# A decoder layer on one core: the diagonal scores and the first score level taken by one series of products

## The reference, cut to what matters

```python
def step(S, inp):
    qc, kc, vc, gc = inp
    b = jnp.cumsum(gc, axis=2)
    o_inter = jnp.einsum('bhtk,bhkv->bhtv', qc * jnp.exp(b), S)
    diff = b[:, :, :, None, :] - b[:, :, None, :, :]
    decay = jnp.where(causal, jnp.exp(jnp.where(causal, diff, 0.0)), 0.0)
    scores = jnp.einsum('bhtk,bhsk,bhtsk->bhts', qc, kc, decay)
    o = o_inter + jnp.einsum('bhts,bhsv->bhtv', scores, vc)
    ...
```

## Time and profile before

| | |
|---|---|
| median of three runs | 1082.59 us |
| the profiled execution's own time | 1080.87 us |
| its span | 1079.1 us |
| TensorE matmul busy | 1051.9 us (97%) |
| VectorE busy | 674.0 us (62%) |
| ScalarE busy | 478.9 us (44%) |
| mean granted clock of TensorE | 0.996 of full |
| first diagonal product | 67.53 us from the start |
| last L255 matmul of the four rounds | 598.8 us |

### The profile page before, as it was taken

How to read it: one execution, slowest core, us unless ns; L and a number is a source line. 1 busy time by engine, 2 the same in 40 slices (tenths; PEclk the granted TensorE clock), 3 DMA queues, 4 the chain that set the end, 5 groups by cost and what they waited for, 6 DMA issues and landing times.

```text
span 1079.1 us, 25184 instructions
## 1 busy us (share of the span) xinstructions
PE 1051.9 (97%) x11040; PEld 992.1 (92%) x11040; DVE 674.0 (62%) x978; ACT 478.9 (44%) x760; POOL 69.8 (6%) x87
## 2 busy tenths in 40 slices
PE   7999999999999999999999979799999999999997
PEld 5999999999999999999999858799999999988886
DVE  6265635675526665356664578988888888744644
ACT  6433344632537333445335527644444444633532
POOL 5100003000013000030000020000000000000000
PEclk9999999999999999999999989999999999999999
DMA  6622223623227222245222363042433323422212
GB/s 192 171 65 79 72 57 116 180 61 80 69 61 216 79 61 79 71 125 166 64 61 89 98 200 104 1 117 79 112 84 92 104 80 98 131 85 78 79 59 87
DMA packets 138717, 105.30 MB, mean 98 GB/s; under 512 B 4017, under 2 KB 123825, under 8 KB 138609
## 3 DMA queue, kind: packets, MB, share of 16 engines
q1 hardware_dynamic: 133744, 85.88, 28.0%
q0 software_dynamic: 4864, 17.83, 5.5%
HBM read 91.89 MB, written 11.80 MB: 96 GB/s over the span
## 4 chain that ended last, share of the span: by engine, by line
PE 93%; DVE 3%; ACT 2%; DVEq 1%; ACTq 0%; issue 0%; DMA 0%; SPq 0%
PE ps L255 43%; PE ps L1805 21%; PE ps L1829 13%; PE ps L362 5%; PE ps L1028 2%; PE ps L1059 1%; PE ps L1049 1%; PE ps L1005 1%; PE ps L1061 1%; PE ps L1066 1%; PE ps L1097 1%; PE ps L1042 1%; PE ps L1024 1%; PE ps L1086 0%; PE ps L1012 0%
## 5 line engine op out<-in xcount | busy, mean ns | idle before, releaser
L255 PE MATMUL ps<-x_hi,w_lo_t 128*128 128x288 f32 x1152 | 251.5, 300 | 0.0
L255 PE MATMUL ps<-x_hi,w_hi_t 128*128 128x288 f32 x1152 | 246.1, 295 | 0.0
L255 PE MATMUL ps<-x_lo,w_hi_t 128*128 128x288 f32 x1152 | 246.0, 295 | 0.0
L241 ACT ACTIVATE w_hi_t<-w_raw_t 128x1024 fp32r<-128x1024 f32 x73 | 77.2, 1058 | 307.6 <-PE ps L255 307.3
L245 DVE TENSOR_TENSOR w_lo_t<-w_raw_t,w_hi_t 128x1024 fp32r<-128x1024 f32 x73 | 89.3, 1223 | 169.1 <-ACT w_hi_t L241 168.7
L255 PEld LDWEIGHTS ps<-x_hi,w_lo_t 128*128 128x128 f32 x1152 | 184.0, 189 | 4.3 <-issue 2.5
L255 PEld LDWEIGHTS ps<-x_lo,w_hi_t 128*128 128x128 f32 x1152 | 185.1, 188 | 0.0
L255 PEld LDWEIGHTS ps<-x_hi,w_hi_t 128*128 128x128 f32 x1152 | 185.1, 188 | 0.0
L1805 PE MATMUL ps<-x_hi,w_lo_t 128*128 128x288 f32 x264 | 78.1, 296 | 3.5 <-DVE work L1621 2.4
L1805 PE MATMUL ps<-x_lo,w_hi_t 128*128 128x288 f32 x264 | 77.8, 295 | 0.0
L1805 PE MATMUL ps<-x_hi,w_hi_t 128*128 128x288 f32 x264 | 77.8, 295 | 0.0
(11 more groups left out here) (302 smaller groups left out, 2106.6 us busy)
## 6 DMA issues: line engine op xcount, KB each, us to landing
w_raw_t<-in_w_in_dram SPq DMA_DIRECT2D x73, 512.0 KB, 3.9
merged<-in_w_ffn_in_dram SPq DMA_DIRECT2D x22, 512.0 KB, 5.2
w_raw_t<-in_w_ffn_in_dram SPq DMA_DIRECT2D x22, 512.0 KB, 4.6
w_raw_t<-in_w_ffn_out_dram SPq DMA_DIRECT2D x22, 512.0 KB, 3.7
h_t<-in_x_prompt_dram SPq DMA_DIRECT2D x8, 512.0 KB, 5.1
h_t<-in_state_gla_dram POOLq DMA_DIRECT2D x4, 1024.0 KB, 6.2
h_t<-in_state_hgrn_dram POOLq DMA_DIRECT2D x8, 512.0 KB, 7.9
out_dram<-h_t POOLq DMA_DIRECT2D x4, 1024.0 KB, 6.0
```

The source lines that it names most:

```text
L241: nc.scalar.activation(w_hi_t[:, u % NSPL, 0:nk, :], w_raw_t[:, u % NRAW, 0:nk, :], ACT.Copy).then_inc(w_hi, 1)
L255: m = nc.tensor.matmul(out[:, q, :], w[:, u % NSPL, k, :], x(k, q), start=first and i == 0, stop=last and i == len(todo) - 1)
```

## The change

The buffers of queries and of decayed queries become two halves of one buffer, QT: Q holds the plain queries, T3 (formerly a separate scratch buffer) the decayed ones. The step "diag" is gone from the table, and the four rounds have 27 steps each in place of 28. VectorE writes T3 = Q times Z in slot 7, behind a wait for the queries (`qk_in`) that TensorE had before. The step "level0" then multiplies each strip of 32 keys with 64 columns: the 32 plain queries and the 32 decayed ones. In slot 8 VectorE takes both results out of the one product in `first_take`: six copies by the identity, a drain, and six copies by the mask of the odd columns, strip by strip; then it frees the bank pair. All later levels and the output products read T3 where they read Q. The scratch uses of Q and T3 change places.

```diff
-NOW = {2: ["decay"], 6: ["diag"], 7: ["level0", "v0"], 8: ["level1", "v1"], 9: ["level2", "v2"],
+NOW = {2: ["decay"], 7: ["level0", "v0"], 8: ["level1", "v1"], 9: ["level2", "v2"],
...
-    Q = A("Q", [P, 3, T])
+    QT = A("QT", [P, 2, 3, T])
+    Q, T3 = QT[:, 0, :, :], QT[:, 1, :, :]
     O = A("O", [P, 4, T])
-    T3 = A("T3", [P, 3, T])
...
-    kblk = [t[:, :, :].rearrange("p a b -> p (a b)")[:, 0:NB * P].rearrange("p (b d) -> p b d", b=NB) for t in (T3, B)]
+    kblk = [t[:, :, :].rearrange("p a b -> p (a b)")[:, 0:NB * P].rearrange("p (b d) -> p b d", b=NB) for t in (Q, B)]
...
-        def diagonal(j):
-
-            s = step(j, "diag")
+        def first_take(j):
+
+            dve.drain()
+            s = step(j, "level0")[:, 0:3 * NT * 2 * STRIP].rearrange("p (h a t) -> p h a t", a=2, t=STRIP)
+            dve.memset(tick[:, :], 0.0)
             one = ident[:, :].bitcast(I32).rearrange("p (o t) -> p o t", o=1)
-            for t in range(0, C, STRIP):
-                strip = slice(t, t + STRIP)
-                got = s[strip, 0:3 * NT * STRIP].rearrange("p (h t) -> p h t", t=STRIP)
-                if t < TS:
-                    dve.copy_predicated(As[strip, :, strip], one[strip, :, strip].broadcast_to([STRIP, 3, STRIP]), got[:, 3 * NC:3 * NT, :])
-                ins = dve.copy_predicated(Am[strip, :, strip], one[strip, :, strip].broadcast_to([STRIP, 3 * NC, STRIP]), got[:, 0:3 * NC, :])
-            freed(ins, j, "diag")
+            m = mask[:, 0, :].bitcast(I32).rearrange("p (o t) -> p o t", o=1)
+            takes = [(slice(t, t + STRIP), out, heads) for t in range(0, C, STRIP)
+                     for out, heads in ((Am, slice(0, 3 * NC)), (As, slice(3 * NC, 3 * NT))) if out is Am or t < TS]
+            for strip, out, heads in takes:
+                dve.copy_predicated(out[strip, :, strip], one[strip, :, strip].broadcast_to([STRIP, heads.stop - heads.start, STRIP]),
+                                    s[strip, heads, 0, :])
+            dve.drain()
+            for strip, out, heads in takes:
+                t = strip.start
+                ins = dve.copy_predicated(out[strip, :, t + 1:t + STRIP:2],
+                                          m[strip, :, t // 2:(t + STRIP) // 2].broadcast_to([STRIP, heads.stop - heads.start, STRIP // 2]),
+                                          s[strip, heads, 1, 1:STRIP:2])
+            freed(ins, j, "level0")
...
                 if n == 7:
+                    dve.wait_ge(qk_in, j + 1)
+                    dve.tensor_tensor(T3[:, :, :], Q[:, :, :], Z[:, :, :], ALU.mult).then_inc(lvl, 1)
+                if n == 8:
                     if j == 0:
                         dve.wait_ge(consts, CONSTS)
-                    diagonal(j)
-                    dve.tensor_tensor(Q[:, :, :], Q[:, :, :], Z[:, :, :], ALU.mult).then_inc(lvl, 1)
-                if 8 <= n < 8 + NL:
+                    first_take(j)
+                if 8 < n < 8 + NL:
                     level_take(j, n - 8)
...
-            elif name == "diag":
-                pe.wait_ge(qk_in, j + 1)
+            elif name == "level0":
+                pe.wait_ge(lvl, j * NL + 1)
                 for a in range(3 * NT):
                     c, h = divmod(a, 3)
                     for t in range(0, tok(c), STRIP):
                         cols = slice(c * C + t, c * C + t + STRIP)
-                        m = nc.tensor.matmul(s[t:t + STRIP, a * STRIP:(a + 1) * STRIP], K[:, h, cols], Q[:, h, cols], start=True, stop=True)
+                        m = nc.tensor.matmul(s[t:t + STRIP, 2 * a * STRIP:2 * (a + 1) * STRIP], K[:, h, cols], QT[:, :, h, cols], start=True, stop=True)
```

More of the change, by code:

```diff
@@ L319, in norm_rows @@
     def norm_rows(j):
-        return [Q[:, i, :] for i in range(3)] if j == G - 1 else [k_flat[:, i * T:(i + 1) * T] for i in range(3)]
+        return [T3[:, i, :] for i in range(3)] if j == G - 1 else [k_flat[:, i * T:(i + 1) * T] for i in range(3)]
     def sqo(j, d):
@@ L328, in rs_two @@
     def rs_two(j):
-        return Q[:, 0:2, :] if j == G - 1 else k_flat[:, 0:2 * T].rearrange("p (a t) -> p a t", a=2)
+        return T3[:, 0:2, :] if j == G - 1 else k_flat[:, 0:2 * T].rearrange("p (a t) -> p a t", a=2)
     def in_parts(j):
@@ L793, in level_next @@
             L = LEVELS[i]
-            q, k = blocks_of(Q, 2 * L), blocks_of(K, 2 * L)
+            q, k = blocks_of(T3, 2 * L), blocks_of(K, 2 * L)
             if 2 * L > SL:
@@ L1024, in do_step @@
                                 m = nc.tensor.matmul(s[up + e:up + e + STRIP, o:o + L], K[:, h, c * C + e:c * C + e + STRIP],
-                                                     Q[:, h, c * C + t + L:c * C + t + 2 * L], start=True, stop=True)
+                                                     T3[:, h, c * C + t + L:c * C + t + 2 * L], start=True, stop=True)
                     else:
@@ L1028, in do_step @@
                             m = nc.tensor.matmul(s[t:t + STRIP, o + t // 2:o + (t + STRIP) // 2], K[:, h, c * C + t:c * C + t + STRIP],
-                                                 second(Q[:, h, c * C + t:c * C + t + STRIP], L), start=True, stop=True)
+                                                 second(T3[:, h, c * C + t:c * C + t + STRIP], L), start=True, stop=True)
                 if L <= 4:
@@ L1034, in do_step @@
                             m = nc.tensor.matmul(s[t:t + STRIP, o + t // 2:o + (t + STRIP) // 2], K[:, h, TP + t:TP + t + STRIP],
-                                                 second(Q[:, h, TP + t:TP + t + STRIP], L), start=True, stop=True)
+                                                 second(T3[:, h, TP + t:TP + t + STRIP], L), start=True, stop=True)
             elif name[:2] == "kt":
@@ L1060, in do_step @@
                     if c > 0:
-                        m = nc.tensor.matmul(s[:, c * C:(c + 1) * C], sp_t[:, c - 1, cols], Q[:, h, c * C:(c + 1) * C],
+                        m = nc.tensor.matmul(s[:, c * C:(c + 1) * C], sp_t[:, c - 1, cols], T3[:, h, c * C:(c + 1) * C],
                                              start=False, stop=True)
@@ L1065, in do_step @@
                     for v in range(0, P, STRIP):
-                        nc.tensor.matmul(s[v:v + STRIP, TP + b * SL:TP + (b + 1) * SL], st[:, v:v + STRIP], Q[:, h, TP + b * SL:TP + (b + 1) * SL],
+                        nc.tensor.matmul(s[v:v + STRIP, TP + b * SL:TP + (b + 1) * SL], st[:, v:v + STRIP], T3[:, h, TP + b * SL:TP + (b + 1) * SL],
                                          start=(b == 0), stop=False, skip_group_check=True)
```

## The result

The changed kernel takes 1086.22 us (median of 8 runs, 1085.55 to 1086.58), the kernel before 1082.36 us (8 runs, 1080.96 to 1083.51). The ratio is 1.0035 with a 95% interval of 1.0024 to 1.0046: 3.9 us slower, and clear of noise.

A forecast was written before the change was run, and what follows sets the result against it. TensorE was taken to bound the four rounds. Per round a wait of 1.6 us less a saving of 0.66 gives +0.94, +3.8 in four; profiled 1080.87 becomes 1084.6, plus 1.7 for the median: 1086.4 us, range 1081.8 to 1090.

The forecast's parts named there:

- What bounds the kernel: In the four rounds TensorE has no slack, so work taken from it or waits added count one for one.
- TensorE's saving: Diagonal step gone, 1.31 us; wider level 0 costs 0.65 more; net 0.66 us a round, 2.6 in four.
- The product with Z: VectorE's product before level 0 ends at 71.9, TensorE arrives at 74.0: room 2.1 us, no wait.
- The release: Level 0's banks, wanted after 6.98 us, are free at 8.5 plus 0.1: TensorE waits 1.6 us a round before level 1.
- The unknown price: Six half copies writing every second element, not in the trace: 1.4, 2.5 or 3.4 us; 2.3 taken.
- My upper bound: Six half copies take 3.4 us if the stride of two on the PSUM side costs another 1.1 ns an element.
- The sum: Wait 1.6 less saving 0.66 gives +0.94 us a round, +3.8 us in four.
- The fast copies: Rival: half copies run at the faster rate, wait 0.7 to 0.8 us cancels the saving, 1083 us; chance 0.20.
- No wait at all: Rival: the twelve copies fit ahead of level 1, only the saving is left, 1080 us; chance 0.08.
- The clock: Rival: idling at the wait lowers TensorE's granted clock, 14 us on top, 1100 us; chance 0.02.
- The useless product: Rival: 64 columns cost twice as much, level 0's change saves only 0.1, 1088.6 us; chance the rest of 0.03.

The follow-up runs named there:

- e1_no_copies: The changed kernel with all twelve copies of the first take left out and the banks freed after a one-element memset; 1079.36 us, ratio 0.9974 to the kernel before.
- e5_narrow: e1_no_copies with level 0 products of only 32 columns, the decayed queries, the plain ones left out; 1076.89 us, ratio 0.9952 to the kernel before.
- e4_dst_plain: The changed kernel with the second six copies writing 16 adjacent elements, not every second one, so scores land in wrong places; 1082.32 us in one run.
- e3_even_odd: The changed kernel with each product's columns streamed even, then odd, so mask copies read PSUM adjacently and identity copies with a stride; 1086.35 us, ratio 1.0045.
- e8_before_keys: The kernel before with only the keys for level 1 written early, in slot 7, into the output buffer; 1081.95 us, ratio 0.9999.

## Why the prediction was right

The forecast was 1086.4 us, the result 1086.22, through the mechanism that was named.

- **What bounds the kernel.** One for one, as the table shows, in both directions: TensorE's work taken away (e1_no_copies, e5_narrow) and TensorE's waits.
- **TensorE's saving.** Forecast 0.66 us a round. The pieces of the chain give 0.58, since level 0 takes 1.82 us and not 1.74; the whole round gives 146.39 - 145.73 = 0.66 (e1_no_copies), and the medians 2.7 us in four against 2.6. By the Trainium skill, TensorEngine Tiling (Array Packing), Instruction Overhead, one column has the same latency as 60, and by that the wider product would have been nearly free. For the rate of a series of products in four groups e5_narrow disagrees, with 0.68 us a round for the second 32 columns.
- **The product with Z.** It ended at 72.48 and level 0 started at 74.59: 2.1 us of room, as forecast. The moved wait for the queries costs nothing: VectorE goes from the split to the product without a gap.
- **The release.** Forecast: first copy 3.35 us after VectorE's start, measured 79.73 - 76.44 = 3.29. Six diagonal copies 2.73, measured 82.43 - 79.73 = 2.70. Six half copies with the last write 2.4, measured 85.08 - 82.50 = 2.58. Wait 1.6, measured 1.67.
- **The unknown price.** I had three sums, 1.4, 2.5 and 3.4 us, and took 2.3, near the one whose form of writing is the same. It was right for the reason given: e4_dst_plain and e3_even_odd separate write and read, and the write carries it all. My upper bound, a further cost of the read of PSUM, doesn't exist here. By the Trainium skill, SBUF — State Buffer, Door 1: The DMA port swizzle, two hits in a line of 16 bytes suffice for full bandwidth; for masked copies that write every second element the trace disagrees, 0.58 us against 0.37.
- **The sum.** Forecast +0.94 us a round, 3.8 us in four; the medians say 3.9. That close a hit is in part luck, because two things that the forecast didn't have nearly cancel. The round grew by 147.50 - 146.39 = 1.11 us, 4.4 us in four, since the wait was 1.67 and not 1.6 and costs 0.1 us more than its length. Against it stands a pause that the kernel before has once, at an output product of round 2. Everything behind it is 0.6 us later than at the same place in the other rounds, and 4.4 - 0.6 = 3.8. It isn't scatter of one execution: e8_before_keys, the only other trace of the queue before, has the same pause (second row), and none of the nine traces of the changed kernel and its versions has it. Its cause stays open.

```profile
457.27 0.30 PE L1069 MATMUL ps<-As,v_t 128*32 128x64 f32 x4 [0.34 <-issue]
457.83 0.30 PE L1075 MATMUL ps<-As,v_t 128*32 128x64 f32 x4 [0.34 <-issue]
```

  The two profiled executions, 1080.87 and 1086.15 us, are 5.3 apart and not 3.8. The changed kernel's ended unit 6 some 0.6 us later, before anything that the change touches (its level 0 starts at 74.59, so unit 7 at 68.2, where unit 6 had ended at 67.60 before). It also took 0.8 us longer behind the four rounds, 481.2 us where it was 480.4, and e8_before_keys took 481.4 there. Single executions scatter by 1 to 3 us, so differences of tenths between two profiles are read place by place, not from the span.
- **The rivals.** The fast copies fell with 0.58 us. No wait at all fell with 1.67 us, four times. The clock stayed at 1.00 through idle times of 1.67 us. The useless product fell with e1_no_copies.

## What to carry to other kernels

When a change merges two products, ask what it does to the reader of the result: here 0.6 us of TensorE were saved a round, and 3.2 us more of VectorE's copies (5.35 us where there were 2.12) moved into a stretch with 1.5 us of room, while the engine idled 4 us just before. Measure the room from the end of the product to the moment its banks are asked for, and put into it only what the release needs; the split and the keys could stand elsewhere, and with both moved the same change gained 0.24% on the kernel before. The busy share of an engine says nothing about this: VectorE was at 62% before and after.

## What the runs showed of the hardware

- A masked copy (COPY_PREDICATED) that writes every second f32 element takes 580 ns for 192 elements on each of 32 partitions, one that writes adjacent ones 368 ns. A tensor product over every second element (L806, 864 elements, 1.06 us) shows no such cost against one over adjacent elements (L920, 1728 elements, 1.95 us), and the pattern of the PSUM read none either (590 and 580 ns in both forms).
- Products of 32 stationary and 64 moving columns start one record in 56 ns on each group of 32 PSUM partitions, whether the other groups work or not: 14 ns a record with four groups in turn, 28 with two, 56 on one group in a row. All 108 records together took 1.80 us, and 5.57 us in the other order. Width from 16 to 32 columns was free (10.1 and 10.4 ns a record), from 32 to 64 it was not.
- A wait of TensorE for VectorE costs some 0.1 us beyond its length (1.77 us for 1.67, 0.63 for 0.56).
- A stride of two in the moving operand of these products costs little but something: 1.89 us in the chain against 1.82 for 54 products.
